# A hybrid layer on one core: the u columns projected from x times g, the norm's factor applied afterwards

## The chip, the cores and the metric

The kernel runs on one core of a Trainium2 chip. Its time is the device time of one execution in microseconds; three executions of the kernel before took 1927.74, 1927.94 and 1932.67 us, median 1927.94.

## The reference

Two transformer layers run one after the other on 512 tokens of width 1024, in float32. Only the head of the first layer is touched by the change:

```
n = rmsnorm(h, g_mix)             # h * rsqrt(mean(h*h) + 1e-6) * g_mix, per token
z = n @ w_in                      # 1024 -> 7168
q, k, v = 12 heads of 128 each    # columns 0..11, 12..23, 24..35 in blocks of 128
u       = next 512 columns        # blocks 36..39, input of a state-space model
gates   = last 2048 columns       # blocks 40..55
q, k = partial_rotary(q), partial_rotary(k)     # first 32 of each head's 128
attn = dilated, banded attention of q, k, v in three groups of four heads
y    = gelu(s5_ssm(u, ...))       # complex diagonal scan, 32 groups of 16 channels
h    = h + (gate_attn * (attn @ w) + gate_ssm * glu(y)) @ w_out
```

The norm's factor rsqrt(...) is one number per token, so it can be taken out of the product: (x·r·g) @ w = r · ((x·g) @ w).

## The kernel before, in words

Activations lie transposed: 128 features by 512 tokens in a tile, eight tiles for a width of 1024. Every weight product is made of three float32r products: a number is split into a high part (rounded, "hi") and a low part (the rest, "lo"), for weights and for activations, and hi·hi, hi·lo and lo·hi are summed in one bank of PSUM. `blk` issues these three for one block of 128 by 128 weights (L248 to L250), and `proj` issues the blocks k = 0 to 7 of one output column m; `proj2` interleaves two columns block by block, waiting for each activation tile as it is made.

The weights come as a stream of chunks of eight blocks, in the order in which TensorE's program uses them. SyncE's queue loads a chunk into one of four raw buffers (L2211), ScalarE writes its hi into one of three buffers (`prep`, L753), and VectorE writes its lo (`prep`, L1280). A raw buffer is free when the lo four chunks before is made, a hi buffer when TensorE has used the chunk three before. `prep(b)` in an engine's program brings it to two chunks beyond block b. There is no planner: each engine's program is written out by hand as a list, and everything stands in it in a fixed order; an instruction that waits holds up all that is behind it on its engine.

The head of the kernel runs like this. SyncE loads the small vectors, the eight tiles of x and then the first chunks. ScalarE squares each x tile (`square`, L763), VectorE adds the squares up (`add_up`, L1294), TensorE sums over the features with a vector of ones (`total`, L267), VectorE makes the variance (L1298), GpSimd the power -0.5 (`root`, L2016), VectorE a diagonal (L1302) and TensorE spreads it over the partitions of bank 7 (`spread`, L273). Then `scaled` makes the eight n1 tiles: VectorE multiplies x, g and the factor in bank 7 (L1315), ScalarE makes the high part (L780), VectorE the low one (L1307). TensorE projects u first: columns 36 and 37 interleaved into banks 0 and 1, then 38 and 39 into the same banks once ScalarE has copied them out (L793) in another order of elements. SyncE stores u to memory and loads it back in the layout of the scan.

Then a loop over a = 0 to 16 projects q, k and v of head a, one column after the other into alternating banks, and mixes in the attention of head a - 1 (`score` begins in the middle of q's column of a = 1 and needs `rope(0)`) and the steps of the state-space model. VectorE's program between the n1 tiles and `rope(0)` (L1445 to L1450) holds the setup: the angles of the rotary table (L1367, L1368 and the helper's L1334 to L1342), whose sine and cosine ScalarE makes (L785, L787) ahead of the copies of u and of q; exponentials (L1371 to L1380); masks (L1382, L1383); constants of the state-space model (L1387 to L1435). GpSimd's program holds, behind `root`, the powers of the state matrix and then the state-space tables, which wait for VectorE's constants.

## Time and profile before

| | us |
|---|---|
| median of three runs | 1927.94 |
| the profiled execution | 1931.13 |
| its span | 1929.3 |
| TensorE busy | 1859.4 (96%) |
| VectorE busy | 1051.3 (54%) |
| ScalarE busy | 748.1 (39%) |
| GpSimd busy | 260.2 (13%) |
| one hi of a chunk on ScalarE (mean of 286) | 1.055 |
| one lo of a chunk on VectorE (mean of 267) | 1.257 |
| mean granted clock of TensorE | 0.98 of full |

A chunk of weights is a transfer of 512 KB, an x tile one of 256 KB, the small vectors one of 206.5 KB.

The page and the rows name engines PE (TensorE), PEld (its weight loads, which overlap with its products), DVE (VectorE), ACT (ScalarE), POOL (GpSimd) and SP (SyncE). Times are in microseconds from the start of the span. An engine's busy time says little about a short stage: there one reads the timeline, and what each engine waited for. The duration that is shown for a product overlaps with the next one; the distance between two starts is what a product costs in a run of them.

### The profile page before, as it was taken

The page shows a single profiled execution, that of the slowest core. Times are in us where ns is not written, and L with a number is a line of the kernel's source. Part 1 is how long each engine was busy: PE and PEld are TensorE (multiplying, and loading weights), DVE is VectorE, ACT ScalarE, POOL GpSimd, SP SyncE. Part 2 cuts the span into 40 slices and gives each one's busy share as a digit, 9 for nine tenths or more (in the row PEclk, how much of TensorE's full clock was granted, in tenths as well). Part 3 has the DMA queues.
Part 4 walks back from the last instruction along what each step waited for, and adds up shares of the span by engine and source line. Part 5 has one row for each costly group of instructions (what it writes and reads, how often), then busy time and mean ns, then how long its engine had stood idle before and what let it go on. Part 6 is the DMA issues. An engine that isn't in the chain of part 4 may idle for free.

```text
span 1929.3 us, 20889 instructions
## 1 busy us (share of the span) xinstructions
PE 1859.4 (96%) x8140; PEld 1452.8 (75%) x8140; DVE 1051.3 (54%) x1562; ACT 748.1 (39%) x1181; POOL 260.2 (13%) x351
## 2 busy tenths in 40 slices
PE   5999999999999999999989999899999899999997
PEld 4888888777877888888867777666667688888885
DVE  7555454454556544553467594455545466435543
ACT  4454454442344222222343553345444244324431
POOL 7644551100000000000001140211110000000000
PEclk9999999989999999999989999999999899999998
DMA  4322222214334545552323223312104223332321
GB/s 170 115 67 88 87 67 91 88 56 142 98 124 164 178 162 187 185 184 87 126 66 115 82 67 104 125 33 72 44 22 160 86 77 89 97 99 90 96 87 56
DMA packets 64186, 199.31 MB, mean 103 GB/s; under 512 B 7124, under 2 KB 11476, under 8 KB 64088
## 3 DMA queue, kind: packets, MB, share of 16 engines
q1 hardware_dynamic: 64088, 197.97, 31.6%
q8 instruction: 65, 1.06, 0.2%
q14 instruction: 33, 0.27, 0.0%
HBM read 189.55 MB, written 8.39 MB: 103 GB/s over the span
## 4 chain that ended last, share of the span: by engine, by line
PE 70%; issue 20%; DVE 7%; ACT 2%; DMA 0%; POOL 0%; POOLq 0%; DVEq 0%; SPq 0%; ACTq 0%
PE bank L248 20%; PE bank L250 19%; PE bank L249 19%; PE bank L597 2%; PE bank L623 2%; PE bank L610 1%; PE bank L505 1%; DVE tile L1776 1%; DVE tiler L1307 1%; PE bank L277 1%; PE bank L317 1%; PE bank L333 1%; DVE wlo L1280 1%; ACT whi L753 1%; PE bank L395 1%
## 5 line engine op out<-in xcount | busy, mean ns | idle before, releaser
L248 PE MATMUL bank<-tiler,whi 128*128 128x512 f32 x2272 | 923.6, 407 | 15.1 <-DVE tiler L1307 5.3
L249 PE MATMUL bank<-tiler,whi 128*128 128x512 f32 x2272 | 902.7, 397 | 0.0
L250 PE MATMUL bank<-tiler,wlo 128*128 128x512 f32 x2272 | 902.5, 397 | 0.0
L753 ACT ACTIVATE whi<-raw 128x1024 fp32r<-128x1024 f32 x286 | 301.1, 1055 | 654.9 <-PE bank L250 649.3
L248 PEld LDWEIGHTS bank<-tiler,whi 128*128 128x128 f32 x2272 | 432.1, 190 | 139.1 <-issue 28.9
L250 PEld LDWEIGHTS bank<-tiler,wlo 128*128 128x128 f32 x2272 | 431.7, 190 | 101.8
L1280 DVE TENSOR_TENSOR wlo<-raw,whi 128x1024 fp32r<-128x1024 f32 x267 | 334.5, 1257 | 315.8 <-ACT whi L753 315.6
L249 PEld LDWEIGHTS bank<-tiler,whi 128*128 128x128 f32 x2272 | 432.4, 190 | 96.7 <-issue 2.9
L2016 POOL TENSOR_TENSOR stat<-stat,scl 128x4 f32<-128x4 f32 x7 | 7.9, 1130 | 1162.0 <-DVE stat L1298 725.8
L1954 DVE SCALAR_TENSOR_TENSOR tile<-bank,sm,tile 128x511 f32<-128x511 f32 x44 | 33.0, 750 | 98.4 <-ACT tile L1254 61.9
L2007 POOL TENSOR_TENSOR wlo<-raw,whi 128x1024 fp32r<-128x1024 f32 x19 | 45.5, 2397 | 257.9 <-ACT whi L753 257.9
L1307 DVE TENSOR_TENSOR tiler<-tile,tiler 128x512 fp32r<-128x512 f32 x109 | 73.6, 686 | 8.8 <-ACT tiler L780 4.4
L763 ACT ACTIVATE tile<-tile 128x512 f32<-128x512 f32 x45 | 28.4, 630 | 99.5 <-DVE tile L1984 39.7
L1664 DVE CUSTOM_DVE_ANT_0 wide<-wide 128x1024 f32<-128x1024 f32 x48 | 58.5, 1219 | 0.0
L1149 ACT ACTIVATE wide<-bank,stat 128x512 f32<-128x512 f32 (+1 forms) x64 | 33.5, 525 | 46.6 <-DVE stat L1872 46.6
L1872 DVE TENSOR_REDUCE stat<-bank 128x1 f32<-128x512 f32 (+1 forms) x64 | 30.7, 489 | 34.5 <-PE bank L599 33.0
L597 PE MATMUL bank<-tile 96*128 96x384 f32 (+7 forms) x128 | 47.4, 466 | 0.5 <-issue 0.5
L1984 DVE SCALAR_TENSOR_TENSOR tile<-bank,mod,tile 128x512 f32<-128x512 f32 x16 | 11.9, 751 | 62.9 <-PE bank L250 62.9
L623 PE MATMUL bank<-tile 128*64 128x512 f32 (+3 forms) x128 | 45.0, 452 | 0.4 <-ACT tile L1162 0.4
L1693 DVE TENSOR_TENSOR tile<-tile,bank 128x512 f32<-128x512 f32 x22 | 15.1, 688 | 43.3 <-PE bank L250 40.7
L1254 ACT ACTIVATE tile<-bank,sm 128x512 f32<-128x512 f32 x22 | 17.1, 778 | 53.3 <-PE bank L250 53.3
L267 PE MATMUL bank<-ones,tile 128*128 128x1 f32 x64 | 12.4, 320 | 25.2 <-DVE tile L1294 25.2
(341 smaller groups left out, 1573.1 us busy)
## 6 DMA issues: line engine op xcount, KB each, us to landing
raw<-wst SPq DMA_DIRECT2D x286, 512.0 KB, 3.6
wide<-wadaT SPq DMA_DIRECT2D x48, 512.0 KB, 3.5
tile<-xT SPq DMA_DIRECT2D x16, 256.0 KB, 5.2
spare<-tile SPq DMA_DIRECT2D x16, 256.0 KB, 2.0
tile<-spare SPq DMA_DIRECT2D x16, 256.0 KB, 5.5
out<-tile SPq DMA_DIRECT2D x8, 256.0 KB, 2.0
tile<-gblk SPq DMA_DIRECT2D x5, 256.0 KB, 4.7
us<-tile SPq DMA_DIRECT2D x4, 256.0 KB, 4.7
```

What stands on the lines that cost most here:

```text
L248: e.matmul(bank, whi[:, o:o + 128], hi, start=start, stop=False)
L249: e.matmul(bank, whi[:, o:o + 128], lo, start=False, stop=False)
L250: e.matmul(bank, wlo[:, o:o + 128], hi, start=False, stop=stop).then_inc(*sig("blk", n))
L597: e.matmul(bk[:, 0:w], F(QM[h % 2])[K, n * 128:(n + 1) * 128], F(KM[h % 2])[K, 0:w], start=True, stop=True, skip_group_check=True)
L623: e.matmul(B[7][rows_, c0:512], F(VS[h // 8][kb])[:, vo:vo + 64], F(PTM[(4 * h + kb) % 3])[:, c0:512], start=kb == 0, stop=True, skip_grou ...
L753: e.activation(whi[:, c % NHL * W:(c % NHL + 1) * W], raw[:, c % NRAW * W:(c % NRAW + 1) * W], ACT.Copy).then_inc(*sig("hi", c))
L1149: e.activation(prob(h, n), B[3 + (n + 1) % 2][:, 0:w], ACT.Exp, bias=stat[:, ST_MM + z + n:ST_MM + z + n + 1], accum_out=stat[:, ST_MD + z ...
L1280: e.tensor_tensor(wlo[:, h:h + W], raw[:, c % NRAW * W:(c % NRAW + 1) * W], whi[:, h:h + W].bitcast(F32), SUB).then_inc(*sig("lov", c))
L1307: e.tensor_tensor(R(lo), src, R(hi).bitcast(F32), SUB).then_inc(*sig("oplo", name, k))
L1664: e.tensor_tensor_reduce(w, w, F(CR, 2), 1.0, 0.0, MUL, ADD, F(PART)[:, m:m + 1]).then_inc(*sig("ada", m))
L1954: then(e.scalar_tensor_tensor(out=F(t)[:, 1:512], in0=bk[:, 0:511], scalar=col("fcw", 44 + mt), in1=F(t)[:, 1:512], op0=MUL, op1=ADD))
L2007: e.tensor_tensor(wlo[:, h:h + W], raw[:, c % NRAW * W:(c % NRAW + 1) * W], whi[:, h:h + W].bitcast(F32), SUB).then_inc(*sig("log", c))
```

## The change

The u columns are projected from x·g, without the norm's factor. For each x tile as it arrives ScalarE makes the high part of x·g and VectorE the low one, into eight new pairs of tiles. TensorE first multiplies 14 small products of ones, then works through the eight tiles of x·g, with four blocks each, one for each of the u columns, into banks 2 to 5. Only after these 32 blocks does it issue `total` and `spread` of the norm. ScalarE copies the spread factor from bank 7 into a tile, and VectorE multiplies each u bank by it as it writes the u tiles; ScalarE's copies of u fall away.

The columns of q and k of head 0 are interleaved with `proj2` as the n1 tiles are made, and v of head 0 follows. The adds of the squares move from VectorE to GpSimd. SyncE loads chunks 0 to 2 between the x tiles, and chunks 3 and 4 before the constants. The conversions of chunks 0 to 3 stand between the x·g tiles, those of 4 and 5 between the n1 tiles. The reload of u waits until the sine is made. The small angles of the state matrix are made on VectorE after the third x·g tile. VectorE's other setup keeps its place behind the n1 tiles, now with the four u products and chunk 6 ahead of it.

```diff
@@ tensor
             e.wait_ge(*at("ones"))
+            for _ in range(14):
+                e.matmul(B[7][:, 0:128], ones[:, :], ones[:, :], start=True, stop=True)
+            for k in range(8):
+                e.wait_ge(*at("oplo", "xg", k))
+                for j in range(4):
+                    proj("in", 36 + j, B[2 + j], XG, [k])
             total("n1", 59, B[6])
             spread("n1", 60, B[7])
-            proj2("in", 36, B[0], "in", 37, B[1], N1, "n1")
-            for j in (2, 3):
-                e.wait_ge(*at("u", j - 2))
-                proj("in", 36 + j, B[j - 2], N1)
...
+                    if a == 0 and part < 2:
+                        if part == 0:
+                            proj2("in", 0, B[0], "in", 12, B[1], N1, "n1")
+                        continue
                     e.wait_ge(*free_a(s - 2))
+                    if a == 1 and part == 0:
+                        e.wait_ge(*at("u", 3))
@@ scalar
-            for k in range(8):
-                e.wait_ge(*at("io%d" % k, 0))
-                square("n1", k, F(X_RAW[k]), 59, (60, 61))
+            for k in range(9):
+                if k < 8:
+                    e.wait_ge(*at("io%d" % k, 0))
+                    e.activation(R(XG[k][0]), F(X_RAW[k]), ACT.Copy, scale=col("g_mix", k)).then_inc(*sig("ophi", "xg", k))
+                if k in (0, 2, 4):
+                    prep(4 * k - 2 * CB)
+                if k:
+                    square("n1", k - 1, F(X_RAW[k - 1]), 59, (60, 61))
...
-            prep(-CB)
+            prep(CB)
...
+                    if name == "n1" and k in (1, 5):
+                        prep((k // 4 + 2) * CB)
             halves("n1", 8, (62, 63, 65), N1)
-            prep(8)
+            e.activation(F(RBS), B[7], ACT.Copy).then_inc(*sig("rb_sb"))
+            prep(4 * CB)
...
-            for j in range(4):
-                if j >= 2:
-                    start_of("in", 36 + j)
-                e.wait_ge(*made("in", 36 + j))
-                e.activation(F(U[j]).rearrange("p (r c) -> p c r", r=4), B[j % 2].rearrange("p (c r) -> p c r", r=4),
-                             ACT.Copy).then_inc(*sig("u", j))
@@ vector
-            e.wait_ge(*at("dt"))
-            then(e.tensor_tensor(ang, aim, dt, MUL))
-            sincos("ang", ang, tmp)
-            e.wait_ge(*at("sq", "n1", 0))
-            for k in range(1, 8):
-                add_up("n1", k, 59, (60, 61))
+            for k in range(8):
+                hi, lo = XG[k]
+                e.wait_ge(*at("ophi", "xg", k))
+                e.scalar_tensor_tensor(out=R(lo), in0=F(X_RAW[k]), scalar=col("g_mix", k), in1=R(hi).bitcast(F32), op0=MUL,
+                                       op1=SUB).then_inc(*sig("oplo", "xg", k))
+                if k in (0, 2, 4):
+                    prep(4 * k - 2 * CB)
+                if k == 2:
+                    e.wait_ge(*at("dt"))
+                    then(e.tensor_tensor(ang, aim, dt, MUL))
+                    sincos("ang", ang, tmp)
+            prep(CB)
             variance("n1", B[6], 1024, ST_1)
-            prep(-2 * CB)
             e.wait_ge(*at("ident"))
             diagonal("n1", ST_1, 60)
-            prep(-CB)
             scaled("n1", 8, X_RAW, lambda k: col("g_mix", k), B[7], (62, 63, 65), N1)
+            for j in range(4):
+                e.wait_ge(*made("in", 36 + j))
+                if j == 0:
+                    e.wait_ge(*at("rb_sb"))
+                e.tensor_tensor(F(U[j]).rearrange("p (r c) -> p c r", r=4), B[2 + j].rearrange("p (c r) -> p c r", r=4),
+                                F(RBS).rearrange("p (c r) -> p c r", r=4), MUL).then_inc(*sig("u", j))
+            prep(4 * CB)
...
-            start_of("in", 38)
+            start_of("in", 24)
...
-            start_of("in", 39)
+            prep(first.get(("in", 24), 0) + CB)
...
-            start_of("in", 0)
@@ gpsimd
+            for k in range(1, 8):
+                e.wait_ge(*at("sq", "n1", k))
+                if k > 1:
+                    e.wait_ge(*at("acc_n1", k - 1))
+                e.tensor_tensor(F(59), F(59), F(60 + k % 2), ADD).then_inc(*sig("acc_n1", k))
             e.wait_ge(*at("half"))
             root("n1", ST_1)
@@ sync
                 e.dma_start(F(X_RAW[k]), xT[k]).then_inc(*sig("io%d" % k, 0, by=16))
+                if k in (0, 2, 4):
+                    chunks(k // 2 + 1)
             e.dma_start(ident[:, :], consts[:, 0:128]).then_inc(*sig("ident", by=16))
-            chunks(2)
+            chunks(4)
...
+            until("in", 24)
+            e.wait_ge(*at("sin", 1))
             load_u(0)
```

## Rows read from the trace of the kernel before

**Rows 1.** The page, its first part: busy time, share of the span, instructions.
```profile
PE 1859.4 (96%) x8140; PEld 1452.8 (75%) x8140; DVE 1051.3 (54%) x1562; ACT 748.1 (39%) x1181; POOL 260.2 (13%) x351
```

**Rows 2.** Windows: stretch, length, busy us by engine, PEclk, DMA share, GB/s.
```profile
0.00:21.30 21.30, 3.91 (x10) 2.28 (x10) 12.07 (x27) 11.30 (x17) 9.70 (x27) 1.00 0.87 308
...
70.40:400.00 329.60, 327.07 (x1707) 270.72 (x1705) 166.62 (x209) 164.16 (x308) 122.73 (x181) 0.99 0.26 80
```

**Rows 3.** Timeline of the head: start, us, engine, line, operation [idle before <-releaser].
```profile
5.74 1.36 ACT L763 ACTIVATE tile<-tile 128x512 f32<-128x512 f32 x2 [1.12 <-DMA tile<-xT]
...
6.48 5.47 DVE L1294 TENSOR_TENSOR tile<-tile 128x512 f32<-128x512 f32 x7 [0.86 <-ACT tile L763]
...
12.09 1.84 PE L267 MATMUL bank<-ones,tile 128*128 128x1 f32 x8 [12.09 <-DVE tile L1294]
...
14.28 1.85 POOL L2016 TENSOR_TENSOR stat<-stat,scl 128x4 f32<-128x4 f32 x1 [10.54 <-DVE stat L1298]
...
17.02 2.08 PE L273 MATMUL bank<-tile,ones 128*128 128x512 f32 x2 [3.09 <-DVE tile L1302]
...
19.13 1.41 DVE L1315 SCALAR_TENSOR_TENSOR tile<-tile,sm,bank 128x512 f32<-128x512 f32 x2 [1.02 <-PE bank L273]
...
21.32 0.79 PE L248 MATMUL bank<-tiler,whi 128*128 128x512 f32 x1 [2.23 <-DVE tiler L1307]
```

**Rows 4.** Waits of TensorE up to 400 us: total, times, longest.
```profile
PE bank L248 <- ACT tile L793: 3.5, 1, 3.5
```

**Rows 5.** Timeline of TensorE: first full-speed product, and the first score product.
```profile
41.38 0.39 PE L248 MATMUL bank<-tiler,whi 128*128 128x512 f32 x1
...
69.97 0.38 PE L317 MATMUL bank<-tile 128*128 128x128 f32 x2
```

**Rows 6.** Timeline of VectorE from the n1 tiles' end to rope(0)'s.
```profile
29.55 0.52 DVE L1367 CAST tile<-tile 128x512 f32<-128x512 int32 x1
...
35.88 2.82 DVE L1280 TENSOR_TENSOR wlo<-raw,whi 128x1024 fp32r<-128x1024 f32 x2
38.62 0.37 DVE L1371 TENSOR_TENSOR tile<-sm,tile 128x16 f32<-128x16 f32 x1
...
43.96 1.27 DVE L1280 TENSOR_TENSOR wlo<-raw,whi 128x1024 fp32r<-128x1024 f32 x1
...
54.75 1.22 DVE L1280 TENSOR_TENSOR wlo<-raw,whi 128x1024 fp32r<-128x1024 f32 x1
57.38 1.52 DVE L1280 TENSOR_TENSOR wlo<-raw,whi 128x1024 fp32r<-128x1024 f32 x1 [1.40 <-ACT whi L753]
62.95 1.23 DVE L1280 TENSOR_TENSOR wlo<-raw,whi 128x1024 fp32r<-128x1024 f32 x1 [4.05 <-ACT whi L753]
...
67.35 0.78 DVE L1450 TENSOR_TENSOR tile<-tile 32x512 f32<-32x512 f32 x1
```

**Rows 7.** Windows of the first 6 us; the last number is GB/s.
```profile
0.00:3.00 3.00, 0.00 (x0) 0.00 (x0) 0.17 (x2) 1.28 (x1) 2.47 (x9) 1.00 0.39 101
3.00:6.00 3.00, 0.00 (x0) 0.00 (x0) 1.75 (x10) 1.11 (x3) 0.74 (x1) 1.00 0.96 304
```

**Rows 8.** A restart of TensorE in its timeline, and two windows with the clock.
```profile
37.63 0.54 PE L248 MATMUL bank<-tiler,whi 128*128 128x512 f32 x1 [3.51 <-ACT tile L793]
...
38.00:39.00 1.00, 1.00 (x4) 0.81 (x3) 1.00 (x2) 1.00 (x2) 1.00 (x2) 0.50 0.52 160
...
1915.00:1916.00 1.00, 0.64 (x3) 0.64 (x4) 0.31 (x1) 0.00 (x0) 0.00 (x0) 0.65 0.00 0
```

**Rows 9.** GpSimd: the powers' durations (ns min/median/max), and two rows of its timeline.
```profile
L2016 POOL TENSOR_TENSOR stat<-stat,scl x7: 1006/1007/1855, 14.3 to 1917.5; 128x4 f32<-128x4 f32 x7
...
107.56 0.23 POOL L2102 COPY tile<-tile 64x64 f32<-64x64 f32 x1 [25.06 <-ACT tile L834]
...
146.01 1.29 POOL L2148 TENSOR_TENSOR tile<-tile 128x512 f32<-128x512 f32 x1
```

**Rows 10.** ScalarE's copies of u: ns min/median/max.
```profile
L793 ACT ACTIVATE tile<-bank x4: 1050/1116/1137, 36.5 to 50.6; 128x512 f32<-128x512 f32 x4
```

More of the change, by code:

```diff
@@ L62 @@
         "roped": "ropes ropeq ropek",
-        "ssm_dve": "ssm_t scan yt lam",
+        "ssm_dve": "ssm_t scan yt lam u",
         "turned": "bTp vtr ptr0 ptr1 rows"}.items():
@@ L112 @@
 X_RAW = range(51, 59)
+XG, RBS = [(22, 23), (24, 25), (26, 27), (28, 29), (67, 68), (69, 70), (71, 72), (73, 74)], 66
 N1 = [(2 * k, 2 * k + 1) for k in range(8)]
@@ L264, in total @@
             def total(name, acc, bank, last=7):
-                e.wait_ge(*at("acc", name, last))
+                e.wait_ge(*(at("acc_n1", 7) if name == "n1" else at("acc", name, last)))
                 for j in range(4):
@@ L1318, in scaled @@
                         low(name, k - 1, F(w[(k - 1) % len(w)]), *ops[k - 1])
+                    if name == "n1" and k in (2, 6):
+                        prep((k // 4 + 2) * CB)
             def modulated(name, rb, w, ops, so, sh):
```

10 lines of the change are left out of this document (3 added, 7 removed).

## The prediction

> **What bounds the kernel now.** I read the page first: TensorE is busy for 96% of the span [rows 1], so a microsecond in which it stands still early is a microsecond of the total, unless something later was going to wait anyway. Then the busy time by stretch: before 21.3 us TensorE is busy for only 3.91 us, and from 70.4 to 400 us for 327 of 330 us [rows 2]. The change works in the first 70 us only, so the question is when TensorE, having done the same work, comes out at the other end.
>
> The timeline of the head shows one chain: eight x tiles arrive, ScalarE squares, VectorE adds (seven adds, 6.48 to 11.95 us), the total on TensorE at 12.09, the variance, GpSimd's power at 14.28, the diagonal, the spread at 17.02, and the first n1 tile starts on VectorE at 19.13; the first product of u follows at 21.32 [rows 3]. From the start of the total to the first n1 tile are 7.04 us. The waits show one stop after that: the third u column waits 3.5 us for ScalarE's copy of the first, which stood behind the sine of an angle that VectorE made [rows 4].
>
> The row that decides is the first score product, at 69.97 us [rows 5]. It needs rope(0), which ends on VectorE at 67.35 + 0.78 = 68.13 us, 1.8 us earlier. VectorE's queue from 29.55 us to there is the setup (angles of the rotary table, exponentials, masks, state constants) with seven low-part conversions of weight chunks between, and in it only 1.40 + 4.05 us of idle time, both behind ScalarE's high parts [rows 6]. So VectorE's spare time ahead of the first score is 5.45 + 1.8 = 7.3 us. It is the second bound of this stage, nearly level with TensorE, and no average over the kernel (VectorE 54%) tells it.
>
> **The change, part by part.** Time is counted from the start of the span; "lo" is a VectorE low-part conversion of a weight chunk and "hi" ScalarE's high part.
>
> *Start of u.* Chunk 0 now follows sm and x0 in the queue: 0.21 + 0.26 + 0.52 = 1.0 MB. At 101 and 304 GB/s the transfers brought 0.30 MB by 3 us and 1.2 MB by 6 us [rows 7], so 1.0 MB is through at about 5.3 us; x1 (0.73 MB, by the same rates 4.5 us) was usable at 5.74 [rows 3], so about 1.1 us after its bytes. Chunk 0 is usable near 6.4, its hi (1.06 mean, the page) ends at 7.5, its lo (1.22 at 54.75 us [rows 6]) at 8.8 us. The x·g tiles cost some 0.68 on ScalarE, as a square does, and 0.7 on VectorE, as a scaled tile does [rows 3], and are there earlier. u starts at 8.8, not 21.3.
>
> *The u products.* 32 blocks of 3 products are 96. From 41.38 to 69.97 us are 123 products without a stop [rows 5]: 0.232 us each, so 22.3 us, to 31.1. The later operands keep ahead: 3.9 MB are through with x7, which even at 304 GB/s makes it usable at 16 us; ScalarE's sixteen tiles of 0.68 and three hi of 1.06, 14.1 us from 4 us on with some waiting for x, end near 19.5, chunk 3's hi (behind a table load and two sines) near 22, its lo at 23.4, and TensorE asks for it at 8.8 + 72 × 0.232 = 25.5.
>
> *The clock, the first place for a page.* After 3.5 us of standing still the products from 37.63 to 41.38 us took 0.425 us each (nine of them, +1.7 us), and the granted clock of 38 to 39 us reads 0.50, that is 1.2 GHz; the run of products after 41.38 us is at 2.4 GHz [rows 5, 8]. At the end of the kernel the microsecond after a stop of 2.2 us reads 0.65, the level changing within it [rows 8]. The fourteen products of ones are a quarter of a spread each, 0.52 us at the low level (2.08 for the spread at 17.02 [rows 3]) or half of that, 0.26, at the high one; begun at 1 us they end between 6.3 and 8.3 us, and 0.5 to 2.5 us stay idle before u. I count u at full clock; the other end is +1.7 us.
> The Trainium skill, "TensorE: Matmul & The Clock Gate", Part 1, says that the array starts at half clock and that activity alone releases it, which speaks for the products of ones; it says as well that idleness brings half clock back, which speaks against an early u with holes behind it. By the first alone u ends at 31.1, by the second it may be 32.8 and every later restart pays again; the trace agrees with the second at 37.63 us.
>
> *The adds on GpSimd.* A 128x512 tensor operation takes it 1.29 us [rows 9], against 0.78 a piece on VectorE [rows 3]. The second square is ready near 11 us; seven adds at 1.35 from there, with the squares waiting on them in turn, end near 21 us. At twice the price they end at 30, and the last squares, which wait for them, would hold up chunk 3's hi and with it u by some 3 us. That is late against 12, but the total now stands in TensorE's queue behind all 96 products, so it costs nothing below 31 us. If the products were not ahead it would cost 9 us, 21 against 12.
>
> *The norm chain.* Total at 31.3 (last product drained). Eight narrow products at full clock, estimated at half of the 1.84 us that they took at 12.09; the rest as in rows 3. So 7.04 − 0.9 = 6.15 us: the first n1 tile starts at 37.5 us, 18.4 later than now. Ends: 35.6 if GpSimd's first power takes the usual 1.0 [rows 9] instead of 1.85 and the spread runs at full clock, 39.2 with the slow u.
>
> *VectorE behind it.* This is the step that costs. Everything that stood behind the first n1 tile still stands there:
> - n1 tiles: 19.13 to 29.55, 10.4 us [rows 3, 6], now with chunks 4 and 5 between, 2 × 1.24, and a short wait for each hi: 13.0, to 50.5.
> - four u products with a strided write. ScalarE's copies in the same order of elements took 1.12 [rows 10], VectorE's contiguous reads of a bank 0.70 [rows 3]: 2.8 to 4.5. The order of elements is the nearer row, so I take 4.4, to 54.9.
> - lo of chunk 6, 1.2; angles, 29.55 to 35.9, 6.4 [rows 6]: to 62.5.
> - exponentials and masks, 38.62 to 43.96, 5.3; lo of 7 and 8, 2.4; state constants, 43.96 to 54.75 less the two lo that start and interrupt them, 8.4; lo of 9, some 2 us into them, 1.2; rope(0), from the end of the lo of 62.95, 64.2 to 68.1, 3.9 [rows 6]: to 83.7. Chunk 9's hi can be had only once v's column is done, and that makes the next point worth working out.
> - ScalarE's cosine waits for the angles and the two copies of q stand behind it: 62.5, 0.65 for the cosine (a square's time) and 1.1 for the copies (one strided copy of rows 10, as an estimate) make 64.2. TensorE's v column waits for bank 0, which that copy frees; it is idle from about 55 (q and k end near 37.5 + 17.7, paced by VectorE and the two chunks), runs v from 64.2 with a slow start (5.6 + 1.7) to 71.5, so chunk 9's hi ends at 72.6, 0.3 us after VectorE comes for it. rope(0) ends at 84.1.
>
> TensorE has done the first half of the next column by 71.5 + 2.8 = 74.3 and waits 9.8 us for rope(0). The first score is at 84.1 instead of 70.0: +14.1 us, and with the slow restart of 1.7, as at 37.63, **+15.9 us**. GpSimd's powers start behind the same root, 18 us later, and its state work waits for VectorE's constants, 25 us later; it stood idle for 25 us ahead of its second round (up to 107.56 [rows 9]), and TensorE, 16 us later itself, asks for its first result near 118. I count it at nothing; without that cover it would be up to 9 us more. SyncE passes u's stores after VectorE's product, in time for chunk 10. ScalarE loses four copies; nobody waits for that.
>
> Sum on the profiled execution's own time: span 1929.3, time 1931.1, so 1947.0. That execution was 3.2 us above the median of 1927.94, so the median comes to **1943.8 us**, 0.8% slower. A difference of under 0.3% (5.8 us) can't be told from none here.
>
> **The rivals.**
> *Earlier products pay (faster).* If VectorE's setup were not what the first score waits for, TensorE alone would count: q and k at 55.2, v at 60.8, half a column at 63.6, 6.4 us before now, 1921.5 us. For it: TensorE idles 17.4 of the first 21.3 us [rows 2], and 22 us of products move there. Against it: it decides only if rope(0) ends before 63.6, and I have it 20 us later, of terms read from rows. 5%.
> *The late score is caught up (no change).* Somewhere behind 70 us TensorE would have to wait for a thing that keeps its own pace, a transfer say. In the stretch behind it TensorE waits for 2.5 of 330 us, and the transfers take 0.26 of theirs [rows 2], so nothing there keeps a pace of its own. A third of the loss repaid gives 1938, all of it 1928. 5% for under 5.8 us of difference.
> *Half the loss.* VectorE's operations run faster without TensorE and GpSimd beside them, the u products at 0.75, the power at 1.0, the clock high at each restart: 15.9 − 1.4 − 0.85 − 1.0 − 1.7 − 1.0 = 9.9 us, 1938. 15%.
> *More than the loss.* The clock low in u (+1.7), chunk 0 later by 0.8, and the state work on GpSimd uncovered by some microseconds: 1948 to 1952. 13%.
> *The change does not do what it says* (u starts no earlier because chunk 0 is late) would need chunk 0 after 21 us; the rates of rows 7 exclude it.
>
> **How the numbers follow.** My forecast about 1943.8 has 62%, from 1940 to 1947; with half the loss and more than the loss 90% lie above 1933.7. The terms' own bounds give 1938 to 1949; I widen the lower end to 1936. Faster by over 0.3%: 0.05; within: 0.05; slower: 0.90.
>
> **What would show it.** Right: first u product near 9 us and the total near 31; the first n1 tile near 37; q and k done near 55, then two stops of TensorE, of some 9 us behind ScalarE's copy of q and some 10 us behind rope(0); the first score near 84; from there on the same rows as now, 14 to 16 us later. Wrong: a first score before 75 us; VectorE idle for several microseconds between the u products and rope(0); or a wait for GpSimd's state work after 100 us that is not there now.

## The result

Four executions of the changed kernel took 1947.99 to 1953.22 us, median **1951.05**. Four of the kernel before, run beside them, took 1927.74 to 1932.67, median 1928.95. The ratio is **1.0105 (95% interval 1.0090 to 1.0120)**: slower by 20 us. I had forecast 1943.8 with a range of 1936 to 1949. The direction came as written, and so did the two stops of TensorE in which most of the loss shows; the size was too small, and the median lies 2 us outside the range.

| | before | after |
|---|---|---|
| the profiled execution | 1931.13 | 1950.60 |
| its span | 1929.3 | 1948.8 |
| mean granted clock of TensorE | 0.980 | 0.971 |
| first product of u | 21.32 | 9.88 |
| total of the norm starts | 12.09 | 35.55 |
| first n1 tile starts on VectorE | 19.13 | 39.92 |
| first score product | 69.97 | 86.18 |
| landmark: the first of 24 small products of the same kind | 346.5 | 365.2 |

The landmark is a place that both programs pass in the same form. The +18.7 us that stand there are nearly all of the +19.5 us between the two profiled executions, so the loss happens early and nothing repays it. The landmark's row in the grouped view of the changed kernel (ns min/median/max of one, first and last start):
```profile
L387 PE MATMUL bank<-ident,stat x24: 271/273/273, 365.2 to 373.3; 128*4 128x128 f32 x24
```

The page of the changed kernel, first part, against [rows 1]. TensorE's extra 11.8 us of busy time are the products of ones (5.85) and what the low clock adds.
```profile
PE 1871.2 (96%) x8168; PEld 1462.6 (75%) x8168; DVE 1062.1 (55%) x1567; ACT 748.7 (38%) x1186; POOL 268.8 (14%) x358
```

TensorE's timeline of the changed kernel: start, us, line, operation, and in brackets the idle time before it and what ended it. These are all its stops of over 1 us up to the first score, with the total between them, against [rows 3, 5].
```profile
1.05 5.85 PE L284 MATMUL bank<-ones 128*128 128x128 f32 x28 [1.05 <-DVE ones L1356]
9.88 0.77 PE L249 MATMUL bank<-tiler,whi 128*128 128x512 f32 x1 [2.98 <-DVE wlo L1289]
21.36 0.50 PE L249 MATMUL bank<-tiler,whi 128*128 128x512 f32 x1 [1.39 <-DVE tiler L1365]
35.55 0.95 PE L268 MATMUL bank<-ones,tile 128*128 128x1 f32 x8
38.76 1.13 PE L274 MATMUL bank<-tile,ones 128*128 128x512 f32 x2 [2.25 <-DVE tile L1311]
44.62 0.76 PE L249 MATMUL bank<-tiler,whi 128*128 128x512 f32 x1 [4.74 <-DVE wlo L1289]
65.76 0.79 PE L249 MATMUL bank<-tiler,whi 128*128 128x512 f32 x1 [7.02 <-ACT tile L896]
86.18 0.80 PE L319 MATMUL bank<-tile 128*128 128x128 f32 x2 [9.37 <-DVE tile L1470]
```
The last two rows are the two stops that the prediction named, 7.02 us behind ScalarE's copy of q and 9.37 us behind `rope(0)` (9 and 10 were written). The third row was not predicted. Read it as a sign, not as a price: 1.39 us is only what was left of a larger delay on VectorE, since u's first products were slow themselves.

VectorE of the changed kernel, where that delay arises. Stretch 12 to 21 us, the ten small operations of the state matrix's angles (a product with the time step and nine of the helper), and the low part of the fourth x·g tile behind them.
```profile
12.34 1.26 DVE L1371 TENSOR_TENSOR tile<-sm,tile 128x16 f32<-128x16 f32 x1
13.64 0.17 DVE L1345 TENSOR_SCALAR tile<-tile 128x16 f32<-128x16 f32 x1
13.85 1.21 DVE L1346 TENSOR_SCALAR tile<-tile 128x16 f32<-128x16 f32 x1
15.09 1.62 DVE L1348 SCALAR_TENSOR_TENSOR tile<-tile 128x16 f32<-128x16 f32 x3
16.74 1.19 DVE L1349 TENSOR_SCALAR tile<-tile 128x16 f32<-128x16 f32 x1
17.97 0.17 DVE L1351 TENSOR_SCALAR tile<-tile 128x16 f32<-128x16 f32 x1
18.18 1.19 DVE L1352 SCALAR_TENSOR_TENSOR tile<-tile 128x16 f32<-128x16 f32 x1
19.41 0.17 DVE L1353 TENSOR_SCALAR tile<-tile 128x16 f32<-128x16 f32 x1
19.49 1.82 DVE L1365 SCALAR_TENSOR_TENSOR tiler<-tile,sm,tiler 128x512 fp32r<-128x512 f32 x1
```
The same form takes 0.17 us in one row and 1.2 in the next: 16 elements a partition are never 1.2 us of work. The block takes 7.15 us (12.34 to 19.49). GpSimd's timeline says what runs beside it:
```profile
11.77 10.69 POOL L2051 TENSOR_TENSOR tile<-tile 128x512 f32<-128x512 f32 x7 [8.03 <-ACT tile L771]
```
Seven adds from 11.77 to 22.46 us, one behind the other. That they cause it is still a guess here; e9 and e3 below test it.

Behind the norm, VectorE's timeline of the changed kernel shows the queue that the prediction summed up:
```profile
36.54 0.16 DVE L1307 TENSOR_SCALAR stat<-bank 128x4 f32<-128x4 f32 x1 [9.28 <-PE bank L268]
...
39.92 1.41 DVE L1324 SCALAR_TENSOR_TENSOR tile<-tile,sm,bank 128x512 f32<-128x512 f32 x2 [1.22 <-PE bank L274]
...
52.63 3.92 DVE L1384 TENSOR_TENSOR tile<-bank,tile 128x512 f32<-128x512 f32 x4
...
57.52 0.62 DVE L1389 CAST tile<-tile 128x512 f32<-128x512 int32 x1
...
75.28 1.23 DVE L1289 TENSOR_TENSOR wlo<-raw,whi 128x1024 fp32r<-128x1024 f32 x1 [1.37 <-ACT whi L761]
...
85.23 0.90 DVE L1470 TENSOR_TENSOR tile<-tile 32x512 f32<-32x512 f32 x1
```
The first row holds a number that the next experiments use: VectorE stands still for 9.28 us while TensorE works off u. From the first n1 tile at 39.92 to the end of `rope(0)` at 86.13 it then has 46.2 us of work, nearly in one piece. The angles, exponentials, masks and constants in it need no norm.

Windows of the changed kernel: length, busy us by engine, granted clock, DMA share, GB/s. The first is the start of u, the second what follows the first score.
```profile
10.00:11.00 1.00, 1.00 (x3) 0.81 (x4) 1.00 (x2) 1.00 (x2) 0.00 (x0) 0.50 1.02 414
86.00:90.00 4.00, 3.82 (x11) 3.00 (x12) 1.25 (x4) 0.00 (x0) 3.77 (x8) 0.50 0.00 0
```
Both are at the low level, 1.2 GHz, after stops of 2.98 and 9.37 us.

### The profile page after: what moved, and what is told of

It reads as the page before. It is cut to its first block, busy times and chain, and to the rows that moved or that the text cites. A ratio compares the mean times of both kernels' runs of the same rounds, so it can differ in the third digit from the quotient of the medians.

```text
span 1948.8 us, 20957 instructions
## 1 busy us (share of the span) xinstructions
PE 1871.2 (96%) x8168; PEld 1462.6 (75%) x8168; DVE 1062.1 (55%) x1567; ACT 748.7 (38%) x1186; POOL 268.8 (14%) x358
## 4 chain that ended last, share of the span: by engine, by line
PE 69%; issue 20%; DVE 8%; ACT 2%; DMA 0%; POOL 0%; POOLq 0%; SPq 0%; DVEq 0%; ACTq 0%
PE bank L249 19%; PE bank L251 19%; PE bank L250 19%; PE bank L605 2%; PE bank L631 2%; PE bank L618 1%; PE bank L513 1%; DVE wlo L1289 1%; PE bank L319 1%; DVE tile L1796 1%; ACT whi L761 1%; DVE tiler L1316 1%; PE bank L278 1%; PE bank L335 1%; PE bank L397 1%
## 5 line engine op out<-in xcount | busy, mean ns | idle before, releaser
L1158 ACT ACTIVATE wide<-bank,stat 128x512 f32<-128x512 f32 (+1 forms) x64 | 33.5, 525 | 46.6 <-DVE stat L1892 46.6
L1713 DVE TENSOR_TENSOR tile<-tile,bank 128x512 f32<-128x512 f32 x22 | 15.1, 688 | 43.3 <-PE bank L251 40.7
L1727 DVE TENSOR_TENSOR tile<-tile,bank 128x512 f32<-128x512 f32 x16 | 11.0, 687 | 46.8 <-PE bank L251 46.8
```

The costliest lines, as they stand in the source:

```text
L1158: e.activation(prob(h, n), B[3 + (n + 1) % 2][:, 0:w], ACT.Exp, bias=stat[:, ST_MM + z + n:ST_MM + z + n + 1], accum_out=stat[:, ST_MD + z ...
```

## The experiments

All times in the table are medians; each ratio is to the kernel before, run beside it on the same chip. The kernel before had medians of 1932.95 (9 runs), 1930.57 (7) and 1930.89 (15) in the three studies, so ratios and positions in the traces are compared, not medians across studies. The columns are the start of the total, of the first n1 tile, of the first score and of the landmark, from each profile. Behind the landmark all these profiled executions take between 1580.2 and 1585.9 us (1583.6 in the changed kernel, 1580.2 to 1582.5 in most of the experiments on it), a difference that no edit here was meant to make and that has no name. The experiments' ratios, taken against the changed kernel's, stand 2.6 to 4.6 us lower than their landmarks would put them, in all but e6 and c3. So what an edit did in the head is read from the positions, not from the ratio.

| kernel | time | ratio (95%) | total | n1 | score | landmark |
|---|---|---|---|---|---|---|
| before | 1928.95 | 1 | 12.09 | 19.13 | 69.97 | 346.5 |
| after | 1951.05 | 1.0105 (1.0090–1.0120) | 35.55 | 39.92 | 86.18 | 365.2 |
| e1_angles_early | 1942.18 | 1.0061 (1.0040–1.0082) | 35.90 | 41.21 | 79.80 | 359.3 |
| e2_total_early | 1942.52 | 1.0059 (1.0040–1.0078) | 26.81 | 34.34 | 80.46 | 359.5 |
| e7_rope_first | 1938.24 | 1.0036 (1.0024–1.0049) | 36.82 | 41.19 | 78.08 | 354.6 |
| e8_q_copy_first | 1947.72 | 1.0083 (1.0068–1.0098) | 35.65 | 40.96 | 85.55 | 363.9 |
| e9_small_angles_first | 1945.03 | 1.0071 (1.0056–1.0086) | 33.59 | 37.96 | 84.12 | 363.2 |
| e3_adds_on_vector | 1946.24 | 1.0085 (1.0066–1.0104) | 34.84 | 39.19 | 85.26 | 364.3 |
| e5_24_ones | 1949.05 | 1.0098 (1.0077–1.0118) | 36.62 | 40.99 | 87.47 | 366.8 |
| e6_fill_stops | 1949.24 | 1.0094 (1.0076–1.0111) | 34.76 | 40.07 | 84.59 | 362.8 |
| c1_combined | 1921.12 | 0.9953 (0.9939–0.9966) | 23.58 | 28.44 | 61.65 | 338.7 |
| c2_before_constants_late | 1929.62 | 0.9991 (0.9982–1.0001) | 13.05 | 20.09 | 70.72 | 347.3 |
| c3_after_again | 1950.93 | 1.0103 (1.0088–1.0118) | 34.98 | 39.34 | 85.77 | 365.2 |

**Is it VectorE's queue between n1 and the first score?** Three kernels shorten it by different means. e1 takes the rotary angles out of it and puts them into the 9.28 us in which VectorE stood still:

```diff
+            e.wait_ge(*at("pos1"))
+            then(e.tensor_copy(F(RS1), F(43).bitcast(I32)))
+            then(e.tensor_scalar(F(43), F(RS1), col("if1"), None, MUL))
+            sincos("ang1", F(43), F(44))
             variance("n1", B[6], 1024, ST_1)
...
             prep(4 * CB)
-            e.wait_ge(*at("pos1"))
-            then(e.tensor_copy(F(RS1), F(43).bitcast(I32)))
-            then(e.tensor_scalar(F(43), F(RS1), col("if1"), None, MUL))
-            sincos("ang1", F(43), F(44))
```

> The changed kernel with VectorE's angle block (6.4 us) moved ahead of the norm's variance, into the 9.3 us in which VectorE waits for the total. Theory A (the first score comes when VectorE's queue, started by the late norm, is through): rope(0) ends 6 to 6.5 us earlier, at about 79.8 instead of 86.1 us; ScalarE's cosine no longer holds up the copy of q, so TensorE's stop before v (7.0 us) goes and the stop before the score grows from 9.4 to about 11; the total falls by 6 us, to some 1944 to 1945. Rival B (each stop of TensorE is a loss by itself): the stop before v alone gives back 7 us and the score's stop stays 9.4 us: the same total as A, but the score's stop tells it apart. Rival C (only the place of the total in TensorE's queue matters): no change, 1951.

TensorE's timeline of e1:
```profile
60.41 0.50 PE L249 MATMUL bank<-tiler,whi 128*128 128x512 f32 x1 [0.45 <-ACT tile L896]
79.80 0.80 PE L319 MATMUL bank<-tile 128*128 128x128 f32 x2 [10.77 <-DVE tile L1470]
```
The score stands at the 79.8 us of theory A, 6.4 us earlier than in the changed kernel. That it fits to the tenth is luck: the first n1 tile came 1.3 us later in this run, and VectorE's work from there to `rope(0)` shrank by 7.7 us, from 46.2 to 38.5, the angles' 6.4 and the 1.37 that VectorE had waited for chunk 9's high part. The stop of the v column has shrunk to 0.45 us, since the cosine no longer waits for the angles; the other one grew from 9.37 to 10.77 us, since TensorE comes to it sooner and VectorE alone says when it ends. That speaks against rival B, by which it would have stayed. Of 6.4 us, 5.9 are left at the landmark; the ratio fell by 0.0044, or 8.5 us.

e2 leaves VectorE's program as it is and puts the norm's two steps on TensorE between the x·g tiles:

```diff
                 for j in range(4):
                     proj("in", 36 + j, B[2 + j], XG, [k])
-            total("n1", 59, B[6])
-            spread("n1", 60, B[7])
+                if k == 4:
+                    total("n1", 59, B[6])
+                if k == 6:
+                    spread("n1", 60, B[7])
```

> The changed kernel with the norm's total issued after the fifth of the eight x·g tiles (its adds are ready at 22.5 us) and the spread after the seventh, so that the norm's chain runs beside the last products of u. Theory A: the first n1 tile starts at about 32 instead of 39.9 us, everything behind it on VectorE moves by the same 8 us, the first score comes at 78, the total is 1943. Rival D (VectorE has so much work in the head that an earlier factor finds it busy): VectorE is free from 27.3 us, so D gives under 2 us, 1949 to 1951.

The total started 8.7 us earlier and the first n1 tile 5.6. The row of the first n1 tile in VectorE's timeline of e2 shows where the rest went: the spread itself stood behind two more x·g tiles.
```profile
34.34 1.41 DVE L1326 SCALAR_TENSOR_TENSOR tile<-tile,sm,bank 128x512 f32<-128x512 f32 x2 [4.37 <-PE bank L274]
```
The score moved by 5.7 us with it, and the landmark by 5.7; the 8 us of theory A were too many, for the place of the spread. So all of an earlier norm arrives, and all of VectorE's queue is still between.

e7 keeps the queue's length up to the n1 tiles and takes the state-space constants out from ahead of `rope(0)`:

```diff
             start_of("in", 24)
-            e.wait_ge(*at("sin", 0))
-            e.wait_ge(*at("cos", 0))
-            e.tensor_tensor(bre, mag, cs, MUL)
...
             e.wait_ge(*at("sin", 1))
...
                 if att:
                     top(b, 0)
+                if a == 1:
+                    constants()
```

> The changed kernel with the constants of the state-space model (8.4 us of VectorE's small operations) moved from ahead of rope(0) to behind the first row maximum of head 0, and chunk 9's conversion (1.2, and the 1.4 us wait for its high part) left to its place in the loop. Theory A: rope(0) ends 10 to 11 us earlier, near 75.5, the stop before the score all but goes (TensorE itself is there at 76.8), so the score comes at about 77 and is then bound by the stop before v; total 1951 - 9.3 - 1 for the slow restart = 1941. Rival E (GpSimd's tables, which wait for these constants, then come late): a new wait of TensorE between 100 and 130 us eats part of it, 1943 to 1951.

TensorE's timeline of e7:
```profile
66.91 0.80 PE L249 MATMUL bank<-tiler,whi 128*128 128x512 f32 x1 [8.19 <-ACT tile L896]
78.08 0.38 PE L319 MATMUL bank<-tile 128*128 128x128 f32 x2
```
No stop directly ahead of the score, and the bound there is no longer VectorE but TensorE itself, which had lost its time at 58.7 to 66.9 us. GpSimd, whose tables need these constants, got them later still, and no new stop of TensorE appeared. It is the largest single gain: 0.0069 of the ratio, 13 us. Its profiled run was the slowest of its six (1942.31), so its landmark, 10.6 us earlier than in the changed kernel, is the better guide to what the edit did in the head.

**Would the other stop do as well?** The rival was that the stops add up, so that freeing q's bank early is worth its 7 us too. e8 puts the two copies of q ahead of the sine on ScalarE:

```diff
             prep(4 * CB)
+            e.wait_ge(*made("in", 0))
+            e.activation(F(RN)[0:32, :], B[0][0:32, :], ACT.Copy).then_inc(*sig("qn", 0))
+            e.activation(F(QT[0]), B[0], ACT.Copy).then_inc(*sig("q_sb", 0))
             e.wait_ge(*at("ang1", 0))
```

> The changed kernel with ScalarE's copies of head 0's q ahead of the sine and cosine, so that TensorE need not wait for them before v. Theory A: the stop before v (7.0 us) goes, the stop before the score grows by as much; only the 1.4 us that VectorE waited for chunk 9's high part can come back: total 1949.5 to 1951. Rival B (the stops add up): 7 us faster, 1944.

TensorE's timeline of e8:
```profile
60.29 0.50 PE L249 MATMUL bank<-tiler,whi 128*128 128x512 f32 x1 [0.45 <-ACT tile L802]
71.52 0.77 PE L249 MATMUL bank<-tiler,whi 128*128 128x512 f32 x1 [5.36 <-DVE wlo L1292]
85.55 0.80 PE L319 MATMUL bank<-tile 128*128 128x128 f32 x2 [9.13 <-DVE tile L1473]
```
The v column began 5.5 us earlier and TensorE then waited 5.36 us for a chunk's low part, which stands in VectorE's queue, and 9.13 us for `rope(0)` as before. The stop changed its name and its place. The score moved by 0.6 us; the first n1 tile came 1.0 us later in this run, so VectorE's work from there to `rope(0)` shrank by 1.7 us, 44.5 for 46.2, since its wait for chunk 9's high part had gone. That is all that freeing the bank was worth, not 7. Two stops in a row behind one engine are nearly one stop.

**Where did u's late end come from?** u ended at 35.5 us, not at 31.1. Three theories: the 1.2 us operations of VectorE beside GpSimd's adds (F), a late chunk 0 and a low clock at the start of u (G), and a price of the early work itself that remains without the adds (H). e9 puts the small operations ahead of the adds' time:

```diff
-                if k in (0, 2, 4):
-                    prep(4 * k - 2 * CB)
-                if k == 2:
+                if k == 0:
                     e.wait_ge(*at("dt"))
                     then(e.tensor_tensor(ang, aim, dt, MUL))
                     sincos("ang", ang, tmp)
+                if k in (0, 2, 4):
+                    prep(4 * k - 2 * CB)
```

> The changed kernel with the nine small operations of the state matrix's angles on VectorE (128x16) moved from behind the third x·g tile to behind the first, where GpSimd adds nothing yet. In the changed kernel they took 7.1 us from 12.3 to 19.5 us beside GpSimd's adds, against 2.0 us in the kernel before. Theory F (GpSimd's adds slow VectorE's small operations, the fourth x·g tile is late for it and u stops at 20 us): moved, they take about 2 us, the stop of 1.4 us at 20 goes, u ends at 32.5 to 33.7 instead of 35.5, and the first score and the total come 2 to 3 us earlier, 1948 to 1949. Rival G (u is late for chunk 0 and the low clock at its start): u's end stays within 0.7 us of 35.5, and so does the total.

VectorE's timeline of e9, the same operations as above, and two low parts behind them:
```profile
6.01 0.17 DVE L1345 TENSOR_SCALAR tile<-tile 128x16 f32<-128x16 f32 x1
6.22 0.17 DVE L1346 TENSOR_SCALAR tile<-tile 128x16 f32<-128x16 f32 x1
6.42 0.59 DVE L1348 SCALAR_TENSOR_TENSOR tile<-tile 128x16 f32<-128x16 f32 x3
7.05 0.17 DVE L1349 TENSOR_SCALAR tile<-tile 128x16 f32<-128x16 f32 x1
...
12.12 3.48 DVE L1365 SCALAR_TENSOR_TENSOR tiler<-tile,sm,tiler 128x512 fp32r<-128x512 f32 x2
```
Each is back at 0.17 us and the block at 2.0 (5.81 to 7.85, instead of 7.15), u has no stop in its midst and the total starts at 33.59. The seven kernels whose programs are alike up to there but for e5's number of ones (after, c3, e1, e5, e6, e7, e8) have it between 34.76 and 36.82. From the first product of u to the total are 25.6 to 25.7 us in after, c3, e1, e6 and e8, and 23.94 in e9: 1.7 us less. A later row of this timeline is the same collision on other work, which costs nothing here since TensorE is not waiting for it: GpSimd's adds start at 11.54 us here, and two low parts of 128x512 take 3.48 us where two at 9.42 took 1.41.

A window of e9 in u's midst shows what is left:
```profile
11.00:14.00 3.00, 3.00 (x9) 2.32 (x8) 3.00 (x3) 3.00 (x5) 2.31 (x2) 0.50 1.05 406
```
u runs from 9.65 to 33.59 us without a stop, and 96 products at 0.233 us are 22.4; eight of them, from 10.90 on, took 0.427, which makes the other 1.5. So with VectorE in time, the low clock at the start counts in full.

e3 takes the adds off GpSimd instead:

```diff
@@ vector
                     sincos("ang", ang, tmp)
+                if k > 2:
+                    add_up("n1", k - 2, 59, (60, 61))
+            add_up("n1", 6, 59, (60, 61))
+            add_up("n1", 7, 59, (60, 61))
@@ gpsimd
-            for k in range(1, 8):
-                e.wait_ge(*at("sq", "n1", k))
...
-                e.tensor_tensor(F(59), F(59), F(60 + k % 2), ADD).then_inc(*sig("acc_n1", k))
```

> The changed kernel with the seven adds of squares back on VectorE (0.7 us each), between the x·g tiles, and none on GpSimd. Theory F: VectorE's small operations take 0.17 to 0.2 us again, 2 us instead of 7.1, against 5 us of adds; the fourth x·g tile is ready by about 16 us, u does not stop at 20, ends at 32.5 to 33.7, and the total is 1948 to 1949, although VectorE has more to do. Rival H (the adds were rightly moved, VectorE's head has no room for them): u stops longer than 1.4 us and the total grows by 1 to 3 us, 1952 to 1954.

The small operations stood where they had stood, and in VectorE's timeline of e3 they are short again (one row stands for the ten):
```profile
12.54 0.17 DVE L1345 TENSOR_SCALAR tile<-tile 128x16 f32<-128x16 f32 x1
```
The stop at 20 us is gone as well. So the slowness follows the adds, not the place or the operation; that part of F is shown by e9 and e3 together. But the total came at 34.84, later than F's 32.5 to 33.7 and within the spread of the kernels that keep the adds on GpSimd: in that run the granted clock read 0.50 from 9 to 15 us, and thirteen products of u were slow, 2.5 us in all. Its start at 9.87, 22.4 us of products and these 2.5 make 34.8: the saving on VectorE was lost to the clock. The stretch without any stop speaks against H.

e5, with 24 products of ones for 14, takes the low clock at the start of u away:

```diff
-            for _ in range(14):
+            for _ in range(24):
```

> The changed kernel with 24 products of ones ahead of u instead of 14; they end near 9.5 us, where u starts. Theory F: the clock stays at 2.4 GHz at u's start, the first eight products save 1.5 us, and the stop at 20 us grows by the same 1.5, so that u ends where it did and the total stays 1951 within 1.5. Rival G (u's end follows its start and its clock): u ends 1.5 us earlier and the total falls to 1949.5.

The granted clock read 1.00 from 5 to 16 us, and u began at 9.56. TensorE's timeline of e5 shows why this brought nothing:
```profile
21.01 0.50 PE L249 MATMUL bank<-tiler,whi 128*128 128x512 f32 x1 [2.84 <-DVE tiler L1365]
...
36.62 0.95 PE L268 MATMUL bank<-ones,tile 128*128 128x1 f32 x8
```
Faster products reach the same late tile sooner and wait longer, 2.84 instead of 1.39 us. And behind that longer stop the clock is low after all, as a window of e5 shows:
```profile
22.00:23.00 1.00, 1.00 (x4) 0.74 (x3) 1.00 (x2) 0.24 (x1) 0.10 (x1) 0.50 0.00 0
```
Eight products from 21.64 us on took 0.427 us, and the total came at 36.62, 1.1 us later than in the changed kernel and not where theory F had it. In e7, whose clock did not fall at the start either, it is the same: a stop of 2.86 us, slow products behind it, the total at 36.82. So while the fourth tile is late, TensorE pays for the low clock on one side of it or on the other, and G alone, a clock that is mended without VectorE, gives nothing. No run has both mended and nothing else: e9 and e3 mend VectorE's part and keep the slow start, c1 below has neither.

**What does the clock cost after the long stops?** e6 fills them with 24 and 32 products of ones, whose results nobody uses:

```diff
+                    if a == 0:
+                        for _ in range(24):
+                            e.matmul(B[6][:, 0:128], ones[:, :], ones[:, :], start=True, stop=True)
                     e.wait_ge(*free_a(s - 2))
...
+                    if b == 0 and part == 0:
+                        for _ in range(32):
+                            e.matmul(B[6][:, 0:128], ones[:, :], ones[:, :], start=True, stop=True)
                     if att and part == 0:
                         score(b, 0)
```

> The changed kernel with products of ones in TensorE's two stops: 24 ahead of v (a stop of 7.0 us) and 32 ahead of the first score (9.4 us), their results unused. Theory A: they delay nothing, since VectorE's queue sets both ends; v runs at full clock and so the high part of chunk 9 is there 1 to 1.4 us earlier, for which VectorE waits; the score and the products behind it take 3.0 us less for the high clock. Total 1951 - 4 = 1947, and the distance from the first score to the first transposes of the row statistics falls from 279.0 to 276.3. Rival I (a restart costs the 1.7 us seen at 37.63 in the kernel before): 1948 to 1949, distance 277.5.

The first filler did what it was for: v ran at full clock, VectorE's wait for chunk 9's high part was gone, and from the first n1 tile to the end of `rope(0)` are 44.5 us for 46.2. The second was too short. TensorE's timeline of e6, and a window behind its score:
```profile
74.16 7.31 PE L422 MATMUL bank<-ones 128*128 128x128 f32 x64
84.59 0.49 PE L319 MATMUL bank<-tile 128*128 128x128 f32 x2 [3.12 <-DVE tile L1476]
```
```profile
86.00:87.00 1.00, 1.00 (x5) 0.81 (x4) 0.67 (x3) 0.00 (x0) 0.92 (x3) 0.50 0.07 16
```
3.12 us of standing still were left, and the clock was at its low level again behind them. On what a restart costs, e6 is inconclusive by itself. The other profiles answer it together. From the first score to the landmark are 276.5 us in the kernel before and in e7, 276.6 in c2 and 277.1 in c1, none of which stops directly ahead of the score. In the eight with a stop of 9.1 to 10.8 us there (the changed kernel, c3, e1, e2, e3, e5, e8, e9) they are 278.4 to 279.5, and in e6 with its 3.12 us 278.2. A restart after the long stop costs 1.9 to 3.0 us, some 2.5; 1.7, which I had carried over from a stop of 3.5 us [rows 8], is what e6's short one cost.

**Can the early u be made to pay?** c1 takes what the experiments showed and applies it together: the total behind the fifth x·g tile and the spread behind the sixth, the small angles first, q's copies before the sine, the exponentials behind the first row maximum of head 0, the constants behind the second, and `rope(0)` ahead of chunk 8's low part.

```diff
@@ tensor
+                if k == 4:
+                    total("n1", 59, B[6])
+                if k == 5:
+                    spread("n1", 60, B[7])
@@ vector
                 if att:
                     top(b, 0)
+                if a == 1:
+                    exponentials()
...
                     top(b, 1)
...
+                if a == 1:
+                    constants()
```

> The changed kernel with five orders changed at once: the norm's total after the fifth x·g tile and the spread after the sixth; the state matrix's small angles behind the first x·g tile; head 0's q copied before the sine and cosine; exponentials and state constants on VectorE behind the row maxima of head 0; rope(0) ahead of chunk 8's low part. Theory A: the first n1 tile starts near 30 us; VectorE's queue from there to rope(0) is 46.2 less 8.4, 4.5, 1.2 + 1.2 and 1.4 = 29.5 us; rope(0) ends near 60, TensorE is there at 56 to 57, and the first score comes at about 60 instead of 70.0 in the kernel before: total 9 to 10 us below the kernel before, ratio 0.995. Rival E (the constants moved back hold up GpSimd's tables or the row maxima): new stops of TensorE between 60 and 130 us, ratio 0.997 to 1.002.

TensorE's timeline of c1:
```profile
23.58 1.05 PE L268 MATMUL bank<-ones,tile 128*128 128x1 f32 x8 [0.16 <-POOL tile L2066]
27.38 1.02 PE L274 MATMUL bank<-tile,ones 128*128 128x512 f32 x2
46.34 0.47 PE L249 MATMUL bank<-tiler,whi 128*128 128x512 f32 x1 [1.13 <-DVE wlo L1294]
56.37 0.79 PE L249 MATMUL bank<-tiler,whi 128*128 128x512 f32 x1 [4.21 <-ACT tile L928]
61.65 0.63 PE L321 MATMUL bank<-tile 128*128 128x128 f32 x2
```
The first score stands 8.3 us ahead of where it was before the change. Nothing stops TensorE directly before it, but the stop in the row at 56.37 does count: q's column of the next head waits 4.21 us for ScalarE's copy of k, which stands behind the cosine and the high parts of two chunks, and its twelve products up to the score took some 0.43 us each. So c1 could still gain there. The landmark is 7.8 us earlier, and the time is **1921.12 us, ratio 0.9953 (0.9939 to 0.9966)**, faster than both kernels. The prediction's rival "earlier products pay" had put its price at 1921.5 us and its condition at `rope(0)` ending before 63.6. In c1 `rope(0)` ends at 60.06 us. The condition is met and the time is near the price, but by another path: that rival took the first n1 tile at 37.5 us, and c1, which also has the norm's steps earlier, starts it at 28.44. So c1 shows that early u products can pay, and not that VectorE's setup alone had stood in their way.

The control c2 makes the same move of the constants in the kernel before, without the change:

> The kernel before, with its state constants moved behind the first row maximum of head 0 as in the run of rope(0) first, and nothing else. Theory A: in the kernel before TensorE, not VectorE, sets the first score (69.97 us, with rope(0) done 1.8 us earlier), so the score stays at 70 and the total stays within 0.1% of the kernel before. If VectorE's queue were the bound there too, the score would come up to 9 us earlier, ratio 0.995.

It gives 0.9991 (0.9982 to 1.0001), within what can be told from none, and its score at 70.72 stands directly behind TensorE's own work. `rope(0)` ends at 68.43 us, for 68.13 in the kernel before, though 8.4 us of work had gone from ahead of it: VectorE only waited longer for ScalarE's high parts of chunks, 13.5 us in four waits, for 5.45 in two [rows 6]. Those wait for TensorE in turn, since a buffer of high parts is free only when TensorE has used the chunk three before. So in the kernel before VectorE was not the bound, and moving the constants alone brings nothing. How much of c1's gain needs the early u products stays open all the same. The one stop of the kernel before between the start of u and the first score, 3.51 us and a restart of 1.7 behind ScalarE's sine [rows 4, 8], was left in place by c2 (2.09 us there), and no run moved that copy of u ahead of the sine; by these two rows it could be worth up to 5.2 us by itself, as an estimate. c3 is the changed kernel once more beside them:

> The changed kernel once more, beside the other two on the same chip: ratio 1.009 to 1.012 as in the first measurement; total of the norm near 35.5 us, first score near 86 us.

It repeated the result, 1.0103, with the landmark at the same 365.2 us.

## Why the prediction was right in kind and too small

Its sum was 1947.0 us on the profiled execution's own time, and the changed kernel's profiled execution took 1950.60: 3.6 us more. Step by step, on this ledger:

| step, us | predicted | measured |
|---|---|---|
| u starts | 8.8 | 9.88 |
| u ends | 31.1 | 35.5 |
| total to first n1 tile | 6.15 | 4.37 |
| first n1 tile | 37.5 | 39.92 |
| first n1 tile to the end of `rope(0)` | 46.6 | 46.2 |
| first score | 84.1 | 86.18 |
| restart behind it | 1.7 | 2.5 |
| from there on | 0 | +0.8 |

- **The step that failed is "The later operands keep ahead".** It costed ScalarE's and the transfers' share of the x·g tiles and never laid out VectorE's: two chunks' low parts, ten small operations and the fourth tile's low part. By the prediction's own start and pace TensorE would have asked for that tile at about 17 us, and in the run it asked at 20.0 and got it at 21.3. The adds were costed on GpSimd alone ("it costs nothing below 31 us"), which is right for GpSimd. What they do to the engine beside them was not asked. The total came at 35.55 for 31.3, +4.3 us, and the runs divide it: 1.1 is the later start, since chunk 0's high part ended at 8.5 instead of 7.5; 1.7 is the late tile, which e9 gives back (25.7 to 23.9 us from u's start to the total); and 1.5 is the low clock, which e9 shows uncovered. The last was named as the other end of the u term (+1.7) and then left out of the sum ("I count u at full clock"). Late tile and low clock don't simply add up: with the clock mended alone (e5) the total was no earlier.
  The Trainium skill, "SBUF — State Buffer", section "Who interferes with whom", has the rule that speaks against this move, and I had not weighed it: a VectorE instruction with two inputs from SBUF, or one in a mode that uses both of its port pairs, and a GpSimd instruction that reads SBUF exclude each other, and the one that comes second waits for the whole of the first. This trace agrees (1.2 us where 0.17 are needed, and 0.17 again in e9 and e3). By it, seven adds of 1.29 us [rows 9] can hold VectorE back by up to 9 us, as an estimate.
- **The products of ones** were to end between 6.3 and 8.3 us. Fourteen at 0.26 us from 1 us on would end at 4.6, so the lower end was worked out wrongly; they ended at 6.90 here, and at 5.80 in e1 and e8.
- **The norm chain** was 1.8 us shorter than summed. Its power on GpSimd took 1.02 us and the spread 1.13; the prediction named both as a lower end and took the dearer rows. This hid part of the miss.
- **VectorE's queue** was the step that cost, and it came within 0.4 us: n1 tiles 12.7 us for 13.0, the four u products 3.92 for 4.4 (the bound from ScalarE's strided copy was the nearer one), a wait of 1.37 for chunk 9's high part for 0.3. Errors cancel in that 0.4, and part of it is luck.
- **TensorE's two stops** came in place and order; they are not added up in the ledger, since they end with what VectorE does.
- **GpSimd's lateness** cost nothing, as said. No wait for its tables is there behind 100 us, not even in e7, which delays them more.
- **The restart** was carried from a stop of another length, 0.8 us too little; another 0.8 us lie behind the landmark, within the spread of that stretch in the profiles (1580.2 to 1585.9 us). The granted clock over the whole is 0.971 against 0.980.
- **From the profiled execution to a median** the prediction took off 3.2 us, because before's profiled one stood 3.2 us above the median of three. The 31 later runs of the kernel before have medians of 1930.6 to 1933.0; 1927.94 was a low draw of a kernel whose runs spread over 7 us, and the changed one's profiled execution stood near its median. These 3.2 us are nearly half of the distance from 1943.8 to 1951.05, and no mechanism is in them.

Of the rivals, "half the loss" was wrong: VectorE ran slower, not faster, though the power did take its 1.02 us. "More than the loss" (1948 to 1952, 13%) is where the time fell, and it had two of its three reasons right: the low clock in u and chunk 0's lateness both came. The third did not, there is no wait for GpSimd's state work. What was the largest part in u, the adds beside VectorE, it did not name.

## What to carry to other kernels

Work that is moved ahead on one engine pays only if the engine that the next stage waits for has its own queue moved as well: the early u products cost 20 us with the rest left where it stood, and with the norm's steps, VectorE's setup and ScalarE's copies reordered the kernel is 9 us faster than before. When a stop of the critical engine is to be removed, ask what stands behind it on the releasing engine; one of two stops that end with the same engine was worth 0.6 us at the next common point, not its 7 (e8). And when an operation moves to an idle engine, cost its neighbours in the same stretch, not only the engine that takes it.

## What was not expected of the hardware

- **GpSimd's tensor operations hold up VectorE's smallest ones.** Beside adds of 128x512 a VectorE operation of 128x16 took 1.2 us instead of 0.17, those with a single input too, about every second one; the ten together took 7.15 us instead of 2.0. A low part of 128x512 took 1.82 us, and 0.75 before the adds began; a chunk's low part took 2.31 beside them in e9, and 1.22 before. These delays are all 1.0 to 1.1 us, whatever the size of the operation, a little less than the 1.29 of an add alone [rows 9], which fits a wait for the rest of an add; no run shows the wait itself. The adds lose less: seven took 10.69 us, 1.53 each with their waits, and 12.56 in e9, where longer operations of VectorE stood beside them.
- **The clock behind the products of ones differs from run to run.** With the same 14 of them it was at the low level in the changed kernel from 9 us on, after 2.98 us of standing still, and did not fall in e7, after 3.64 us. Twenty-four of them and 1.29 us of standing still kept it at 1.00 (e5).
- **A product on VectorE that reads a bank and writes in a strided order** took 0.94 us from one to the next (four in 3.75 us), against 0.70 for a contiguous product of another form [rows 3].
